# Stick-breaking attention: diagonal masks as two paired operations a pass instead of four, and the next state-space input product placed ahead of the second pass

## The reference

```python
def stick_breaking_attention(q, k, v):
    ...
        earlier = key_pos[None, :] < t[:, None]
        z = jnp.einsum('bqhd,bshd->bhqs', qi, k).astype(jnp.float32) * scale
        log_fail = jnp.where(earlier, jax.nn.log_sigmoid(-z), 0.0)
        log_between = lax.cumsum(log_fail, axis=3, reverse=True) - log_fail
        w = jnp.where(earlier, jnp.exp(jax.nn.log_sigmoid(z) + log_between), 0.0)
        return jnp.einsum('bhqs,bshd->bqhd', w.astype(v.dtype), v)
```

## Time and profile before

| | us |
|---|---|
| median of 3 runs | 3801.8 |
| lowest, highest | 3793.51, 3805.89 |
| the profiled execution | 3783.65 |
| its span in the profile | 3781.9 |
| TensorE busy, VectorE busy, ScalarE busy, GpSimd busy | 3411.8, 2866.9, 1482.0, 1015.6 |
| mean granted TensorE clock | 0.961 of full speed |

### The profile page before, as it was taken

The page is one execution under the profiler, slowest core; times in us unless marked ns, Lnnn a source line. Parts: engine busy times, 40 slices in busy tenths (PEclk is TensorE's granted clock), DMA queues, the critical chain, the costliest instruction groups (busy, mean ns, idle before and its releaser), DMA issues. The chain is left out here.

```text
span 3781.9 us, 58627 instructions
## 1 busy us (share of the span) xinstructions
PE 3411.8 (90%) x20122; PEld 1982.1 (52%) x20122; DVE 2866.9 (76%) x5232; ACT 1482.0 (39%) x1978; POOL 1015.6 (27%) x742
## 2 busy tenths in 40 slices
PE   7899987978888899999888999889797979999997
PEld 3444643546555556666444446445364646566663
DVE  5765436898989768888847654368989897788887
ACT  4324423335353533333333344223253535333333
POOL 0510100141413124444324101002414141244443
PEclk9999998989999999999998999999899999999998
DMA  5001312586969699999640013126869696999995
GB/s 174 29 1 45 129 42 92 180 298 222 342 214 343 215 395 381 375 387 369 226 145 12 1 56 123 56 84 220 300 224 343 225 332 216 395 378 379 384 368 194
DMA packets 386929, 840.91 MB, mean 222 GB/s; under 512 B 33376, under 2 KB 232032, under 8 KB 386016
## 3 DMA queue, kind: packets, MB, share of 16 engines
q1 hardware_dynamic: 312480, 565.39, 42.2%
q0 software_dynamic: 73728, 268.47, 19.2%
q10 hardware_dynamic: 576, 5.37, 0.4%
HBM read 732.14 MB, written 106.95 MB: 222 GB/s over the span
## 5 line engine op out<-in xcount | busy, mean ns | idle before, releaser
L116 PE MATMUL ps<-xh,wh 128*128 128x384 f16 (+1 forms) x2880 | 1000.5, 347 | 164.5 <-DVE wl L95 75.4
L95 DVE SCALAR_TENSOR_TENSOR wl<-wf,wh 128x1024 f16<-128x1024 f32 x656 | 803.7, 1226 | 393.8 <-ACT wh L89 378.4
L89 ACT ACTIVATE wh<-wf 128x1024 f16<-128x1024 f32 x656 | 690.8, 1053 | 927.5 <-PE ps L1647 527.0
L117 PE MATMUL ps<-xl,wh 128*128 128x384 f16 (+1 forms) x2880 | 999.5, 347 | 0.0
L118 PE MATMUL ps<-xh,wl 128*128 128x384 f16 (+1 forms) x2880 | 997.9, 347 | 0.0
L1645 PE MATMUL ps<-work,wh 128*128 128x384 f16 x2048 | 667.7, 326 | 5.6 <-DVE work L1929 3.7
L1647 PE MATMUL ps<-work,wl 128*128 128x384 f16 x2048 | 667.6, 326 | 0.0
L1646 PE MATMUL ps<-work,wh 128*128 128x384 f16 x2048 | 667.6, 326 | 0.0
L1744 POOL DMA_INDIRECT xT<-urows,small x256 | 370.7, 1448 | 1104.4 <-DVE xT L1804 828.1
L1752 POOL DMA_INDIRECT work<-experts,small x256 | 441.3, 1724 | 600.3 <-DVE work L1938 590.8
L116 PEld LDWEIGHTS ps<-xh,wh 128*128 128x128 f16 x2880 | 286.0, 99 | 415.4 <-issue 90.7
(11 more groups left out here) (347 smaller groups left out, 4116.8 us busy)
## 6 DMA issues: line engine op xcount, KB each, us to landing
wf<-experts SPq DMA_DIRECT2D x512, 512.0 KB, 5.9
wf<-proj SPq DMA_DIRECT2D x144, 512.0 KB, 3.3
gates<-work SPq DMA_DIRECT2D x96, 512.0 KB, 7.5
work<-hid SPq DMA_DIRECT2D x256, 192.0 KB, 4.5
work<-gates SPq DMA_DIRECT2D x256, 192.0 KB, 5.3
hid<-work SPq DMA_DIRECT2D x192, 192.0 KB, 6.3
hid<-small SPq DMA_DIRECT2D x64, 192.0 KB, 6.4
xsave<-xT ACTq DMA_DIRECT2D x2, 2048.0 KB, 6.9
```

Of the source, the lines that this page charges most:

```text
L89: m.nc.scalar.activation(m.wh[:, slot, :], m.wf[:, k, :], ACT.Copy, scale=WS).then_inc(m.high_done, 1)
L95: m.nc.vector.scalar_tensor_tensor(m.wl[:, slot, :], m.wf[:, k, :], WS, m.wh[:, slot, :], ALU.mult, ALU.subtract).then_inc(m.split_done, 1)
L116: m.nc.tensor.matmul(out, wh[:, k, :], xh[:, k, 0:n], start=(k == order[0]), stop=False)
L117: m.nc.tensor.matmul(out, wh[:, k, :], xl[:, k, 0:n], start=False, stop=False)
```

## The change

It does two things. First, VectorE masks the diagonal blocks in two operations instead of four, in both mask steps of each head: the blocks at columns 0 and 512 are one operation, the blocks at 896 and 1024 another, each 128 partitions by 2x128 elements, with the mask read twice through a broadcast. Second, on TensorE `ssm_in(2h+1)` moves from behind the second pass to ahead of it, before the wait for `sb_sp`. What it waits for itself (`ssm_mul`, the turn of group 2h-1) is unchanged.

```diff
@@ tensor
         ssm_in(0)
         for h in range(BH):
             st = h * PER_HEAD
+            ssm_in(st + 1)
             pe.wait_ge(m.sb_sp, h + 1)
...
             last.then_inc(m.sb_t, 1)
             if h == 0:
                 turned_queries(1)
-            ssm_in(st + 1)
@@ vector
+        def mask_diagonals(x):
+
+            later = m.before[:, :].unsqueeze(1).to_broadcast([P, 2, P])
+            for at, apart in ((0, 512), (896, 128)):
+                pair = x[:, at:at + 2 * apart].rearrange("p (a t) -> p a t", a=2)[:, :, 0:P]
+                last = TT(pair, pair, later, ALU.mult)
+            return last
...
-            for s in range(NT):
-                o, _n = sb_cols(s)
-                last = TT(sp_[:, o:o + P], sp_[:, o:o + P], m.before[:, :], ALU.mult)
-            last.then_inc(m.sb_sp, 1)
+            mask_diagonals(sp_).then_inc(m.sb_sp, 1)
...
-            for s in range(NT):
-                o, _n = sb_cols(s)
-                last = TT(wt[:, o:o + P], wt[:, o:o + P], m.before[:, :], ALU.mult)
-            last.then_inc(m.sb_wm, 1)
+            mask_diagonals(wt).then_inc(m.sb_wm, 1)
```

## The result

Five runs of the changed kernel have a median of 3824.6 us (3818.7 to 3831.4), five of the kernel before one of 3801.8 (3793.5 to 3805.9). The ratio is 1.0067, with a 95% interval of 1.005 to 1.0085: 19 to 32 us slower, 22.8 by the medians. The forecast was 3814, range 3792 to 3829, with slower at 0.44 and no change at 0.43.

The account below looks back on a forecast made before the run. A ring of TensorE and VectorE steps per head bounds it, the late engine differing by head. Per layer -0.1 plus 6.6 for the clock gave +6.5, +13 in all: 3796.7 profiled, plus 18.2 to the median, said as 3814, range 3792 to 3829.

Parts of the forecast that it names:

- The masks, -1.0 ahead of the pass and -0.13 behind it: VectorE, each layer: pairing saves 1.0 us ahead of the second pass in heads 1 to 3, 0.13 per weights' masks.
- The masks' gain is lost as slack: From head 2 on TensorE is the late engine, so the 1.0 us saved by the masks ends as slack on VectorE.
- My sum at today's clock, -0.1 a layer: All terms of a layer with the clock held at each operation's present level: 2.58 - 1.0 + 0.5 + 0.4 - 2.58.
- Head 0, +2.58 for the product and about 1.6 for the pass: Head 0: the moved product delays the second pass by 2.58 us; a lower clock level adds about 1.6.
- the 0.5 for the product: Each head: products run partly at the lower level, taken as 0.5 us for each of four, 2 a layer.
- Some idle time stays ahead of head 1's pass: Head 1, TensorE: the moved product fills 2.58 of 4.8 us of idle time; some 2 us stay.
- TensorE is late by 2 us in head 2: Head 2: TensorE needs 16.0 us up to the pass, VectorE's masks 13.9, so the interval grows by 0.5.
- The clock decides, and all four passes begin low: All second passes begin at 1.2 GHz, not two of four, behind two input products: 3 + 1.6 + 2 = +6.6 a layer.
- the low stretch of 10.1 us: Low-clock stretch behind head 2's pass, where group 5's product runs; could go for about -4, taken as staying.
- The tail, -2.58: Behind head 3's pass, the moved product no longer delays output products, values and `ssm_in(8)`: -2.58 us a layer.
- idle time alone: Rival, faster: the clock falls only after idleness, so head 1's pass stays full; up to -21 us in all; chance 0.16.
- "No change": Rival: the level falls where it does today, sum -0.1 a layer, 3801.6 us; chance 0.24.

Follow-up runs that it names:

- table_later: Kernel before the change with GpSimd starting each table one group later, masks and TensorE order unchanged: 3782.3 us against 3796.3, ratio 0.9964.
- dense_filler: Full change plus four unneeded 128-row by 512-column products between the two input products in heads 1 and 3: 3821.2 us, ratio 1.0065 to the kernel before.
- both_not_in_head_0: Full change, but in head 0 the input product of group 1 stays behind the second query product: 3801.1 us, ratio 1.0001 to the kernel before.

## Why the prediction was right, step by step

- *The masks, -1.0 ahead of the pass and -0.13 behind it.* Right: 3.60 became 2.60, 0.90 became 0.76, with one GpSimd operation fewer waited for, as `table_later` confirms from the other side.
- *The masks' gain is lost as slack.* Right in the full change: the passes of heads 1 and 2 start 3.0 and 2.4 us after the masks are done, and the move costs the same without the pairing (21.9 against 22.8). Without the move the gain isn't lost: 7 us. My sum at today's clock, -0.1 a layer, hid that one part was worth keeping.
- *Head 0, +2.58 for the product and about 1.6 for the pass.* The mechanism was right, the size too small in layer 1. The moved product itself took 4.28 us at a clock of 0.54, and the pass 10.98 instead of 7.86, a cost of 3.1. The second query product reaches VectorE at 153.18 instead of 145.13, 7.5 us later beside the 0.6 by which the stage began later, where my terms give 4.7 with the 0.5 for the product. In layer 2 the product took 2.58 and the pass 9.8, and the second query product was 4.1 us later in the stage, a little less than what I had put down. By the runs head 0 is the larger part of the loss, some 21 us of both layers; these direct terms explain about half of that, and the rest comes behind it. The line of before:

```profile
145.13 0.69 DVE L1028 TENSOR_TENSOR work<-ps,cosT 96x512 f32<-96x512 f32 x1 [2.36 <-PE ps L600]
```

- *Some idle time stays ahead of head 1's pass.* Wrong: TensorE reached the pass 3 us after the masks. The values waited for the later masks of head 0 and then ran at the lower level, which I had not carried on.
- *TensorE is late by 2 us in head 2.* Right, 2.4.
- *The clock decides, and all four passes begin low.* Right for layer 1; in layer 2 the fall came as a pass began or within it. `dense_filler` shows it in three passes of four. The term was +6.6 a layer; the stages grew by 13.7 and 10.2. The term that was too small is the one that I took as staying, the low stretch of 10.1 us. There are three such stretches now. From the scores to the next input product heads 0, 1 and 2 of layer 1 take 12.3, 12.7 and 12.7 us where they took 7.1, 9.5 and 14.0, 7 us more in all, 1.9 of them a wait for the masks in head 0. So the upper end of my sum, +11 a layer, was passed in layer 1 (13.7) and by the medians (11.4 a layer). That the result lies in the range owes something to luck: the range ran to 3829, wider than the sum's own end. The stretch of head 0, before (its input product starts at 154.66) and after:

```profile
147.61 2.42 PE L541 MATMUL ps<-work 64*128 64x512 f32 x8
```

```profile
153.07 2.42 PE L541 MATMUL ps<-work 64*128 64x512 f32 x8
157.42 3.50 PE L641 MATMUL ps<-work 128*64 128x512 f32 x8 [1.93 <-DVE work L1087]
...
165.39 0.72 PE L613 MATMUL ps<-work 64*128 64x256 f32 x2
```

- *The tail, -2.58.* Right in full. From the end of head 3's pass to the turn of group 8 it was 13.52 us (227.76 to 241.28) and is 10.94 (244.57 to 255.51), 2.58 less. VectorE's wait there shrank from 4.83 to 2.99 only.

```profile
244.57 0.64 PE L627 MATMUL ps<-work,xl 32*32 32x256 f32 x2
```

- *Rivals.* The level doesn't follow idle time alone: head 0's fell with TensorE busy throughout. The Trainium skill (TensorE: Matmul & The Clock Gate, section Why this matters for your kernels) advises to leave no idle gaps between bursts of matmuls. That isn't enough for this kernel: with the 4.8 us of idle time ahead of head 1's pass filled by a thin product, the pass took 11.39 us where it had taken 10.73. "No change" fell with the passes of heads 0 and 3, at 0.71 and 0.70.

The profiled executions differ by 47.7 us, of which 23.9 lie in the two stages and the rest between and behind them, in parts that the change doesn't touch. The other profiles settle that this rest is spread. Over all twelve profiled kernels the part between the stages takes 1753.8 to 1767.9 us and the part behind them 1663.3 to 1677.9. The kernel before has 1754.3 and 1663.3, at the lower end of both; the changed one has 1765.3 and 1675.5, inside both.

Open: why the level falls in one layer and not in the other behind the same instructions, as in head 0 of `both_not_in_head_0` and head 3 of `dense_filler`.

## What to carry to other kernels

Before filling a gap on TensorE, look at what kind of work goes in and what granted clock the pass behind it gets; a thin product next to another can cost more than it takes itself. And when an operation on VectorE takes four times what its width says, look at GpSimd's timeline first: moving GpSimd's work by one step gained 14.0 us by the medians where halving the number of operations gained 6.8 (the intervals of the two ratios overlap). Try the parts of a change one by one: here one was a gain of 0.2% and the other a loss of 0.5%, and together they were not the sum of the two.

## What the runs showed that I had not expected

Added work can be nearly free: some 14 us more on TensorE left the time as it was, as far as the intervals tell (1.0065 against 1.0067), while three passes of the four behind it took 8.1 us. And the level can fall within a stretch in which TensorE has no idle time at all: in head 0 the first input product ran at 1.00 for 2.6 us, the second one's window has 0.54.
